# Two products of one stationary operand as one matmul of 512 columns, with the halves summed at eviction

## The reference, cut to what matters

```
def swiglu(h, w_gate, w_up, w_down):              # w_gate, w_up: 1024 x 2816
    return (jax.nn.silu(h @ w_gate) * (h @ w_up)) @ w_down

def memory_cross_attention(h, mem_n, w_q, w_kv, q_gain, k_gain, w_o):
    q = rms_norm((h @ w_q).reshape(b, t, 4, 256), q_gain)
    k, v = jnp.split(mem_n @ w_kv, 2, axis=-1)
    k = rms_norm(k.reshape(b, m, 4, 256), k_gain)
...

def diff_attention(h, w_qkv, ...):
    q, k, v = jnp.split(h @ w_qkv, 3, axis=-1)
    q = rms_norm(q.reshape(b, t, 8, 2, 64), q_gain)
    k = rms_norm(k.reshape(b, t, 8, 2, 64), k_gain)
...
```

## Time and profile before

| what | value |
|---|---|
| runs before | 2462.51, 2464.56, 2465.21 us (median 2464.56) |
| the profiled execution, its own time | 2465.9 us |
| its span in the profile | 2464.1 us |
| mean granted TensorE clock | 0.997 of full speed |
| stages in it: first cross attention, feed-forward (gate and up) | about 288 to 318, 359 to 486 us |
| differential projections, second cross attention's projections | about 557 to 629, 688 to 767 us |

### The profile page before, as it was taken

How to read it: one execution, slowest core, us unless ns; L and a number is a source line. 1 busy time by engine, 2 the same in 40 slices (tenths; PEclk the granted TensorE clock), 3 DMA queues, 4 the chain that set the end, 5 groups by cost and what they waited for, 6 DMA issues and landing times.

```text
span 2464.1 us, 38383 instructions
## 1 busy us (share of the span) xinstructions
PE 2414.9 (98%) x15891; PEld 2157.9 (88%) x15891; DVE 1872.7 (76%) x2262; ACT 1450.7 (59%) x1715; POOL 184.1 (7%) x189
## 2 busy tenths in 40 slices
PE   7999999999899999999999999999999999999999
PEld 6878999999798788888888888888889999999997
DVE  6977565546756798889888988898987786586874
ACT  3235554436654677777777777777754565535663
POOL 0200112202010000000000000000000121000220
PEclk9999999999999999999999999999999999999999
DMA  8331445554243699999999999999964455462551
GB/s 242 115 111 37 139 126 188 187 187 156 69 154 113 232 378 358 370 341 371 357 369 336 370 365 369 337 367 370 372 217 135 137 197 180 127 198 86 180 188 52
DMA packets 331027, 565.85 MB, mean 230 GB/s; under 512 B 17624, under 2 KB 172484, under 8 KB 330724
## 3 DMA queue, kind: packets, MB, share of 16 engines
q1 hardware_dynamic: 318182, 555.03, 64.8%
q10 hardware_dynamic: 12670, 8.35, 1.2%
HBM read 562.28 MB, written 2.24 MB: 229 GB/s over the span
## 4 chain that ended last, share of the span: by engine, by line
PE 88%; DVE 6%; ACT 3%; issue 1%; ACTq 0%; DMA 0%; DVEq 0%
PE bank L230 24%; PE bank L232 24%; PE bank L231 24%; PE bank L2340 4%; DVE chunks_lo L360 2%; ACT chunks_hi L351 1%; PE bank L2909 1%; PE bank L3717 1%; PE bank L1899 1%; PE bank L1874 1%; PE bank L709 1%; PE bank L729 1%; PE bank L2332 1%; PE bank L2691 1%; PE bank L3696 1%
## 5 line engine op out<-in xcount | busy, mean ns | idle before, releaser
L3843 DVE TENSOR_TENSOR weight_lo<-ring,weight_hi 128x2048 fp32r<-128x2048 f32 x336 | 766.7, 2290 | 113.3 <-ACT weight_hi L3691 111.9
L3691 ACT ACTIVATE weight_hi<-ring 128x2048 fp32r<-128x2048 f32 x336 | 643.5, 1918 | 209.1 <-PE bank L232 208.8
L360 DVE TENSOR_TENSOR chunks_lo<-ring,chunks_hi 128x2048 fp32r<-128x2048 f32 x167 | 384.7, 2305 | 266.2 <-ACT chunks_hi L351 266.1
L351 ACT ACTIVATE chunks_hi<-ring 128x2048 fp32r<-128x2048 f32 x168 | 320.4, 1907 | 227.7 <-PE bank L232 224.4
L230 PE MATMUL bank<-x_parts,chunks_hi 128*128 128x256 f32 x1408 | 403.4, 286 | 1.5 <-DVE x_parts L445 1.2
L232 PE MATMUL bank<-x_parts,chunks_lo 128*128 128x256 f32 x1408 | 398.4, 283 | 0.0
L231 PE MATMUL bank<-x_parts,chunks_hi 128*128 128x256 f32 x1408 | 398.3, 283 | 0.0
L230 PE MATMUL bank<-weight_hi,xg_hi 128*128 128x512 f32 x896 | 353.4, 394 | 1.6 <-DVE xg_lo L3849 1.6
L232 PE MATMUL bank<-weight_hi,xg_lo 128*128 128x512 f32 x896 | 349.8, 390 | 0.0
L231 PE MATMUL bank<-weight_lo,xg_hi 128*128 128x512 f32 x896 | 349.6, 390 | 0.0
L230 PEld LDWEIGHTS bank<-x_parts,chunks_hi 128*128 128x128 f32 x1408 | 269.9, 192 | 3.8 <-DVE x_parts L445 1.4
(11 more groups left out here) (569 smaller groups left out, 4311.0 us busy)
## 6 DMA issues: line engine op xcount, KB each, us to landing
ring<-in_moe_w_gate SPq DMA_DIRECT2D x112, 1024.0 KB, 6.4
ring<-in_moe_w_up SPq DMA_DIRECT2D x112, 1024.0 KB, 6.4
ring<-in_moe_w_down SPq DMA_DIRECT2D x112, 1024.0 KB, 7.0
ring<-in_w_up SPq DMA_DIRECT2D x44, 1024.0 KB, 5.1
ring<-in_w_down SPq DMA_DIRECT2D x22, 1024.0 KB, 4.9
ring<-in_xa_w_kv SPq DMA_DIRECT2D x16, 1024.0 KB, 5.6
ring<-in_w_in SPq DMA_DIRECT2D x16, 1024.0 KB, 5.4
ring<-in_da_w_qkv SPq DMA_DIRECT2D x12, 1024.0 KB, 5.1
```

What stands on the lines that cost most here:

```text
L351: act.activation(self.home(n)[0], ring[:, c.slot], ACT.Copy)\
L360: dve.tensor_tensor(lo, ring[:, c.slot], hi.bitcast(F32), ALU.subtract)\
L3691: act.activation(weight_hi[:, slot(m, odd + next_)], ring[:, m % ROUND], ACT.Copy).then_inc(weights_hi.sem, 1)
L3843: dve.tensor_tensor(weight_lo[:, at_], ring[:, m % ROUND], weight_hi[:, at_].bitcast(F32), ALU.subtract)\
```

## The change

For the tiles concerned, the two products of the upper weights become one matmul of 512 columns: its moving operand is both parts of x for slice k, its output the whole bank, the product with the upper part on the left and with the lower part on the right. The lower weights by upper x still go to the left half. At eviction DVE adds the two halves with a `tensor_reduce` over an innermost dimension of 2. For k tiles of the cross attention this takes the place of the copy; elsewhere it writes to the destination of the old eviction, DVE waits for itself (`ordered`), and the old operation then runs in place on that. In the feed-forward the wait for the widened gate stands behind the reduction. The tiles concerned are n > 1 in both cross attentions (up to 15), n >= 2 in the feed-forward's gate and up part, 2 < n < 16 in the differential attention; `together3`, the wide v tiles and all other stages stay.

```diff
+        def side_by_side(pe, b, l, x, k, first, last_):
+            pe.matmul(b[:, :].rearrange("p (i t) -> p i t", i=2), l[0], x[:, 0:2, k], start=first, stop=False, skip_group_check=True)
+            return pe.matmul(b[:, 0:T], l[1], x[:, 0, k], start=False, stop=last_, skip_group_check=True)
...
+        def sum_of_halves(dve, out, b):
+            return dve.tensor_reduce(out, b[:, :].rearrange("p (i t) -> p t i", i=2), axis=mybir.AxisListType.X, op=ALU.add)
+        def join_halves(dve, out, b):
+            ordered(dve, dve_own, sum_of_halves(dve, out, b))
+            return out
-        def tile3(pe, c, a, x, ready=None):
+        def tile3(pe, c, a, x, ready=None, halves=False):
...
+                stationary = [v[:, k, a:a + P] for v in w]
+                if halves:
+                    mm = side_by_side(pe, b, stationary, x, k, k == 0, k == DT - 1)
+                else:
+                    mm = three(pe, b[:, 0:T], stationary, [x[:, i, k] for i in range(2)], k == 0, k == DT - 1)
...
@@ cross_attention, PE and DVE
-                        marks.append(tile3(pe, chunk_of(n), n % 2 * P, x_parts, ready if n == 0 else None))
+                        marks.append(tile3(pe, chunk_of(n), n % 2 * P, x_parts, ready if n == 0 else None, n > 1))
...
                     if n < 8:
+                        if n > 1:
+                            src = join_halves(dve, q[:, n], bank[(first + n) % 4])
                         i_ = dve.tensor_tensor(q[:, n], src, x_root, ALU.mult)
                     elif n < 16:
-                        i_ = dve.tensor_copy(k[:, n - 8], src)
+                        i_ = sum_of_halves(dve, k[:, n - 8], bank[(first + n) % 4])
...
@@ swiglu, DVE (up_and_down calls side_by_side for n >= halves_from = 2)
+                        if n >= HALVES:
+                            src = join_halves(dve, gs[:, i % 2], bank[(start + n) % 4])
+                        dve.tensor_tensor(gs[:, i % 2], src, x_root, ALU.mult)\
                            .then_inc(scaled.sem, scaled.tick())
                     else:
-                        dve.wait_ge(widened.sem, widened.at(i + 1))
                         if i >= 2:
                             dve.wait_ge(acts_lo.sem, acts_lo.at(i - 1))
+                        if n >= HALVES:
+                            src = join_halves(dve, prod[:, i % 2], bank[(start + n) % 4])
+                        dve.wait_ge(widened.sem, widened.at(i + 1))
+                        dve.tensor_tensor(prod[:, i % 2], src, sgr[:, i % 2], ALU.mult)\
...
@@ diff_mixer, DVE (PE: tile3 with halves=True for 2 < n < 2 * DT)
+                    if 2 < n < 2 * DT:
+                        src = join_halves(dve, q[:, n] if n < DT else kt[:, n % 4], bank[(first + n) % 4])
```

More of the change, by code:

```diff
@@ L389, in tile3 @@
                     pe.wait_ge(*ready(k))
-                mm = three(pe, b[:, 0:T], [v[:, k, a:a + P] for v in w], [x[:, i, k] for i in range(2)], k == 0, k == DT - 1)
+                stationary = [v[:, k, a:a + P] for v in w]
[3 more added lines that the diff above has]
+                    mm = three(pe, b[:, 0:T], stationary, [x[:, i, k] for i in range(2)], k == 0, k == DT - 1)
             mm.then_inc(tiles_done.sem, tiles_done.tick())
@@ L1000, in up_and_down @@
         def up_and_down(xp, acts, c0, free, ready, after=None, wide=False, begin=None, emptied=None,
-                        by_token=None):
+                        by_token=None, halves_from=None):
             acts_lo = sig("acts_lo")
@@ L1016, in product @@
                         pe.wait_ge(*begin["ready"](k))
-                    mm = three(pe, bank[b][:, 0:T], [v[:, k, n % 2 * P:(n % 2 + 1) * P] for v in w],
-                               [x[:, i, k] for i in range(2)], k == 0, k == DT - 1)
+                    stationary = [v[:, k, n % 2 * P:(n % 2 + 1) * P] for v in w]
+                    if halves_from is not None and n >= halves_from:
+                        mm = side_by_side(pe, bank[b], stationary, x, k, k == 0, k == DT - 1)
+                    else:
+                        mm = three(pe, bank[b][:, 0:T], stationary, [x[:, i, k] for i in range(2)], k == 0, k == DT - 1)
                 if ks[-1] == DT - 1:
@@ L1124, in swiglu @@
             acts_hi, acts_lo = sig("acts_hi"), sig("acts_lo")
-            NT = 2 * FT
+            NT, HALVES = 2 * FT, 2
             def free(pe, n):
@@ L1174, in _ @@
                             dve.wait_ge(gated.sem, gated.at(i - 1))
-                        dve.tensor_tensor(gs[:, i % 2], bank[(start + n) % 4][:, 0:T], x_root, ALU.mult)\
+                        src = bank[(start + n) % 4][:, 0:T]
+                        if n >= HALVES:
+                            src = join_halves(dve, gs[:, i % 2], bank[(start + n) % 4])
+                        dve.tensor_tensor(gs[:, i % 2], src, x_root, ALU.mult)\
                            .then_inc(scaled.sem, scaled.tick())
                     else:
-                        dve.wait_ge(widened.sem, widened.at(i + 1))
                         if i >= 2:
                             dve.wait_ge(acts_lo.sem, acts_lo.at(i - 1))
-                        dve.tensor_tensor(prod[:, i % 2], bank[(start + n) % 4][:, 0:T], sgr[:, i % 2], ALU.mult)\
+                        src = bank[(start + n) % 4][:, 0:T]
+                        if n >= HALVES:
+                            src = join_halves(dve, prod[:, i % 2], bank[(start + n) % 4])
+                        dve.wait_ge(widened.sem, widened.at(i + 1))
+                        dve.tensor_tensor(prod[:, i % 2], src, sgr[:, i % 2], ALU.mult)\
                            .then_inc(multiplied.sem, multiplied.tick())
@@ L1230, in _ @@
                     if 2 < n < 2 * DT:
-                        marks.append(tile3(pe, chunk_of(n), n % 2 * P, x_parts))
+                        marks.append(tile3(pe, chunk_of(n), n % 2 * P, x_parts, halves=True))
                     elif n > 2:
```

4 lines of the change are left out of this document (2 added, 2 removed).

## The result

| | before | after |
|---|---|---|
| runs | 2461.39 to 2465.21 us, median 2463.53 (6) | 2471.86 to 2477.01 us, median 2473.49 (6) |
| profiled execution: its time, span | 2465.9, 2464.1 us | 2472.15, 2470.4 us |
| mean granted clock in it | 0.997 | 0.995 |

The change makes the kernel slower by 9.96 us: ratio 1.004, 95% interval 1.003 to 1.0051, or +7.4 to +12.6 us.

What follows compares the result with a forecast made beforehand. PE leads in the feed-forward, but DVE's loop through ACT sets the cross attentions' pace. Terms 4.4 - 2.8 - 0.2 + 6.5 = +7.9 us on the median of 2464.56 gave 2472.5 us, range 2465 to 2486.

Steps and rivals of the forecast that it cites:

- PE's price of a step: Every changed tile: one matmul of 512 and one of 256 columns save 13.3 ns per step, 8.0 us for 600.
- The rival in which a two-piece operand is no faster: All changed tiles: no gain on PE, +10.9 us, 2475.5 us; no separate chance, within the forecast's own spread.
- The reduction: DVE's evictions: adding the halves, priced by 512 values read, takes 0.69 us; forecast with R 0.6 to 0.8, chance 0.60.
- The dear reduction: Rival at DVE's evictions: a reduction costs 1.22 us, sum +41 us, 2506 us; chance 0.15.
- the cheap one: Rival at DVE's evictions: a reduction costs 0.42 us, sum -0.3 us, 2464.3 us; chance 0.14, with values between.
- Second cross attention: DVE's loop through ACT sets the pace: three q pairs 1.46 longer, four k pairs 0.54 longer, +6.54 us.
- First cross attention: The same DVE loop: three pairs of evictions 1.46 us longer each, +4.38 us, with PE's saving lost in a wait.
- Feed-forward: PE leads: 4.5 us saved on PE, less 1.7 of stall once DVE's loop of 11.59 outlasts its cover: -2.8 us.
- the forecast's 1.7 of stall: Feed-forward: DVE falls 0.49 us behind per round, 4.4 over nine rounds, less cover 2.7, from about tile 30.
- Differential projections: Six rounds 0.73 longer, 4.4 less 1.7 of slack; last square at 610.5, PE there 1.4 us earlier: about -0.2 us.
- The total: Whole kernel: 4.4 - 2.8 - 0.2 + 6.5 = +7.9 us, giving 2472.5 us.

Runs made afterwards that it cites:

- evictions alone: The full change, but the upper part's product is two matmuls of 256 columns again, with DVE's new evictions kept: 2475.11 us.
- matmuls alone: The full change, but DVE evicts only the left half with the old operations, leaving out one product: 2459.88 us.
- feed-forward, cross and evictions alone: Change kept only in the feed-forward, 2462.82 us; only in both cross attentions, 2474.48 us; kernel before 2464.72 us. The third is evictions alone.

## Why the prediction was right

- **PE's price of a step.** Forecast 13.3 ns. With DVE out of the way the feed-forward's round is 11.10 and the stage 4.47 shorter (forecast 11.10 and 4.5). Shown for that stage. The rival in which a two-piece operand is no faster falls. That the price is one number for all streams was wrong: elsewhere a step gives back 13.3 or 6.7 ns. The Trainium skill (TensorE: Matmul & The Clock Gate, Back-to-back issue gap) gives 2.5 ns for the isolated gap of a warm matmul; by it the 336 steps of the feed-forward would have given 0.84 us, an estimate, and this trace does not agree.
- **The reduction.** Forecast 0.69, measured 0.682, and 1.06 from one reduction to the next (724.16 to 725.22), as taken. Shown, and with the reductions doubled a second one costs 0.72 to 0.75 with its wait in all four stages. The dear reduction, 1.22, and the cheap one, 0.42, both fall. The penalty that the Trainium skill gives for accesses which leave a short line each time (SBUF — State Buffer, Door 1: The DMA port swizzle) does not show for DVE reading two values a kilobyte apart in PSUM.
- **Second cross attention.** +6.5, measured +6.47, by rounds of 8.30 and 7.38. Shown by evictions alone (+6.45 without PE's part), and the bound itself by the two kernels with another order on ACT.
- **First cross attention.** +4.4, measured +4.36, with 5.56 of waiting. The attention behind gave 0.36 to 0.5 back, which the sum had not.
- **Feed-forward.** -2.8, measured -2.69, loop 11.59 against 11.56, the first gap at tile 30 as forecast, and 0.3 to 0.5 per four tiles behind it. Of the 4.47 that PE alone would give, 1.78 were lost (forecast 1.7): 1.4 by the four gaps, and 0.4 because 60 of the steps between them ran at the higher price. That the two together meet the forecast's 1.7 of stall so closely is in part luck.
- **Differential projections.** -0.2, measured 0.00. Here two terms were mis-sized, though little hung on them. ACT's last square starts at 611.02 in the kernel after and ends at 611.42, which less the 0.65 by which its stage begins late is 610.8 (forecast 610.5); PE waits 0.62 for it at 611.47. And PE would have been there 0.9 earlier, not 1.4, as more than half of its streams in this stage run at the higher price. With the matmuls alone all of them do, and behind its first sums PE waits for nothing: 104 steps at 6.7 ns are 0.7, and the stage came 0.64 earlier.
- **The total.** The stages sum to +8.6, of which 0.84 lie in the differential attention, where nothing was changed. Windows of the kernel after, behind the first cross attention's projections and in the differential attention (share of the full clock ahead of the last two numbers):

```profile
316.40:323.20 6.80, 3.86 (x8) 2.69 (x9) 4.44 (x10) 2.50 (x6) 0.00 (x0) 0.53 0.47 156
661.20:664.60 3.40, 3.07 (x13) 2.21 (x11) 1.94 (x7) 2.30 (x6) 0.00 (x0) 0.56 0.01 2
```

  and the same stretches of the kernel before:

```profile
317.00:320.40 3.40, 2.69 (x6) 2.18 (x7) 1.97 (x6) 0.75 (x3) 0.00 (x0) 0.54 0.38 129
661.20:664.60 3.40, 2.79 (x19) 2.29 (x18) 1.86 (x6) 2.96 (x9) 0.00 (x0) 1.00 0.00 0
```

  At 661 PE is near 1.2 GHz in the one and at 2.4 in the other; the stretch is there with the matmuls alone and absent in feed-forward, cross and evictions alone, so it isn't tied to a part of the change. Without it the stages sum to +7.8 against the forecast's 7.9. That is a comparison of the stages of two executions, whose spans differ by 6.25, since stretches ahead of the stages and behind them lie otherwise. The medians are 9.96 apart. The interval is wide enough for 7.9 and 9.96, and what the other 2 us are, if anything, stays open.

## What to carry to other kernels

An engine that is busy for 98% of the span and holds 88% of the chain may still be led by another in single stages: the period of a loop on each engine tells who leads, and a saving counts only there. Fewer instructions on PE at the price of a longer eviction pay in a stage with slack at evictions, and a queue order that takes a copy out of the loop (ACT's copy ahead of the square) first makes that slack. A price per step that was read in one stream has to be read again in the streams that the edit makes: broken at each eighth tile, the same steps gave back half. End a stage at the event that its work leads to, here the last sums of squares, ahead of the next stretch at a low clock. And read the sum of the stages and the total apart: one stall far behind the edit took back more than half of a gain that the stages had shown.

## What the runs showed of the hardware that was not expected

- A step of one wide and one narrow matmul has two prices, 0.3467 and 0.3533 us. A stream keeps one of them until it is broken, over 333 steps with matmuls alone.
- A stall of PE of 2.3 us at the same matmul in two executions of one kernel, put down to "issue", ends 1.2 to 1.3 us after a load of 16 KB of instructions; so do two of 0.67 in other kernels, though the program text around the place is the same in all.
- The stretches at 1.2 GHz move. In the kernel after PE stands for 5.56 us up to 319.24, and the clock is low from 316.85 to 323.68, twice as long as the 3.4 us from 317.27 in the kernel before, where PE had waited 0.69. The sums of squares that follow, 1.13 for four at the full clock, took 2.08. All eight kernels in which PE waits for the last squares here, for 0.67 to 7.88 us, have a stretch that begins at 315.3 to 317.9; the four traces in which it does not wait have none. The kernel before with the other order has one of 6.8 us in the differential attention, from 656.4 on and far from its edit, and that attention took 2.25 longer.
- DVE reads two values a kilobyte apart in PSUM in the time of two neighbours: 682 ns for a reduction over 512, 686 for a copy of 512.
